# Input projections of a gated encoder layer: tiles one by one, or two by two as Strassen products

## The reference

```python
h = rms_norm(x, g_pre);  proj = h @ w_in          # 1024 x 7424: 58 tiles of 128 columns
ya = short_gated_conv(a_b, a_c, a_x, w_conv) * silu(a_z);            ua = ya @ w_up_a
yb = window_attention_with_sink(rope(q), rope(k), v) * silu(b_z);    ub = yb @ w_up_b
mk, mv = split(rms_norm(mem, g_mem) @ w_mem_kv)   # mem: 256 tokens
ym = memory_cross_attention(m_q, mk, mv) * silu(m_z);                um = ym @ w_up_m
merged = sigmoid(g0) * ua + sigmoid(g1) * ub + sigmoid(g2) * um
return x + rms_norm(merged @ w_out, g_post)
```

## Time and profile before

| | us |
|---|---|
| median of 3 runs | 1021.28 |
| profiled execution | 1020.34 |
| its span, first to last instruction | 1018.3 |
| TensorE busy | 990.7 |
| VectorE busy | 474.3 |
| ScalarE busy | 347.5 |
| GpSimd busy | 167.6 |

### The profile page before, as it was taken

How to read it: one execution, slowest core, us unless ns; L and a number is a source line. 1 busy time by engine, 2 the same in 40 slices (tenths; PEclk the granted TensorE clock), 3 DMA queues, 4 the chain that set the end, 5 groups by cost and what they waited for, 6 DMA issues and landing times.

```text
span 1018.3 us, 12976 instructions
## 1 busy us (share of the span) xinstructions
PE 990.7 (97%) x4672; PEld 824.7 (81%) x4672; DVE 474.3 (47%) x896; ACT 347.5 (34%) x567; POOL 167.6 (16%) x85
## 2 busy tenths in 40 slices
PE   4999999999999999999999999999999999999997
PEld 3788888888878888888888888888888888887885
DVE  5524322245477777774555544334435312127343
ACT  6321131211365555553320344434422211115121
POOL 1112122121111111111220011121122112210000
PEclk9999999999999999999999999999999999999999
DMA  6322111112111111111121410011111111160322
GB/s 224 107 51 53 62 41 62 41 41 70 32 50 50 50 49 49 49 39 62 41 84 62 135 62 31 31 51 38 44 42 45 49 31 62 31 257 0 124 82 83
DMA packets 21339, 65.41 MB, mean 64 GB/s; under 512 B 3232, under 2 KB 4384, under 8 KB 21056
## 3 DMA queue, kind: packets, MB, share of 16 engines
q1 hardware_dynamic: 20992, 64.39, 19.0%
q10 hardware_dynamic: 320, 0.66, 0.4%
HBM read 56.51 MB, written 4.19 MB: 60 GB/s over the span
## 4 chain that ended last, share of the span: by engine, by line
PE 84%; DVE 7%; ACT 4%; issue 3%; DMA 1%; DVEq 0%; SPq 0%; ACTq 0%
PE pm L377 22%; PE pm L379 22%; PE pm L378 22%; PE pm L617 3%; PE pm L619 3%; PE pm L618 3%; ACT area_a L738 2%; PE sa L466 2%; PE pv L589 1%; PE pm L541 1%; PE sa L573 1%; PE pv L480 1%; DVE area_a L1027 1%; DVE units_r L1034 1%; PE sa L458 1%
## 5 line engine op out<-in xcount | busy, mean ns | idle before, releaser
L377 PE MATMUL pm<-h_hi,units_r 128*128 128x512 f32 x928 | 364.0, 392 | 3.0 <-DVE h_lo L935 2.8
L379 PE MATMUL pm<-h_hi,units_r 128*128 128x512 f32 x928 | 361.7, 390 | 0.0
L378 PE MATMUL pm<-h_lo,units_r 128*128 128x512 f32 x928 | 361.7, 390 | 0.0
L340 POOL TENSOR_TENSOR units_r<-units,units_r 128x1024 fp32r<-128x1024 f32 x80 | 166.4, 2080 | 731.9 <-ACT units_r L638 731.9
L377 PEld LDWEIGHTS pm<-h_hi,units_r 128*128 128x128 f32 x928 | 174.5, 188 | 39.3 <-DVE h_lo L935 3.4
L379 PEld LDWEIGHTS pm<-h_hi,units_r 128*128 128x128 f32 x928 | 174.5, 188 | 36.5
L378 PEld LDWEIGHTS pm<-h_lo,units_r 128*128 128x128 f32 x928 | 174.6, 188 | 35.2
L638 ACT ACTIVATE units_r<-units 128x1024 fp32r<-128x1024 f32 x90 | 91.7, 1019 | 198.1 <-PE pm L379 172.2
L1179 DVE TENSOR_TENSOR area_a<-area_a,pm 128x1024 f32<-128x1024 f32 x15 | 18.3, 1221 | 139.5 <-PE pm L379 139.5
L377 PE MATMUL pm<-y_hi,units_r 128*128 128x512 f32 x192 | 76.9, 401 | 0.0
L379 PE MATMUL pm<-y_hi,units_r 128*128 128x512 f32 x192 | 75.0, 390 | 0.0
(11 more groups left out here) (154 smaller groups left out, 1037.9 us busy)
## 6 DMA issues: line engine op xcount, KB each, us to landing
units<-in_w SPq DMA_DIRECT2D x58, 512.0 KB, 3.3
units<-in_wup SPq DMA_DIRECT2D x24, 256.0 KB, 2.6
area_m<-in_x SPq DMA_DIRECT2D x8, 512.0 KB, 7.0
units<-in_wmem SPq DMA_DIRECT2D x8, 512.0 KB, 3.2
area_a<-in_wout SPq DMA_DIRECT2D x2, 2048.0 KB, 10.5
units<-in_x SPq DMA_DIRECT2D x8, 512.0 KB, 3.9
out<-area_a SPq DMA_DIRECT2D x7, 512.0 KB, 2.9
area_a_r<-area_m SPq DMA_DIRECT2D x16, 128.0 KB, 2.3
```

Source lines behind the costliest of these rows:

```text
L340: nc.gpsimd.tensor_tensor(w_lo[:, p, 0:width], raw[:, p, 0:width], w_hi[:, p, 0:width].bitcast(F32), ALU.subtract).then_inc(lo_made, 1)
L377: pe.matmul(pm[:, p, cols], hi, src_hi[:, k, cols], start=(k == 0), stop=False)
L378: pe.matmul(pm[:, p, cols], hi, src_lo[:, k, cols], start=False, stop=False)
L379: mm = pe.matmul(pm[:, p, cols], lo, src_hi[:, k, cols], start=False, stop=(k == chunks - 1))
```

## The change

The 58 tiles are taken in 29 pairs. For a pair, the weights are a 2x2 arrangement of blocks (A11, A12: first tile, two halves of the 1024 inputs; A21, A22: second tile), and the transposed h is 2x2 as well (B11, B21, B12, B22; 512 by 512 each). Instead of the 8 block products, 7 are made (Winograd's form of Strassen's scheme): P1 = A11 B11, P2 = A12 B21, P3 = S4 B22, P4 = A22 T4, P5 = S1 T1, P6 = S2 T2, P7 = (A11 - A21) T3, with S1 = A21 + A22, S2 = S1 - A11, S4 = A12 - S2 and T1 = B12 - B11, T3 = B22 - B12, T2 = B22 - T1, T4 = B21 - T2. A product is 4 blocks x 3 = 12 matmuls. So:

- At the start seven combinations of h (`hc`) are made and split in place of `h_hi` and `h_lo`; VectorE makes the 16 sums, ScalarE the high parts, GpSimd and VectorE the low parts by turns.
- For each pair VectorE makes the four sums of weight blocks (L1201, L1203, L1209, L1217; 128x512, from SBUF to SBUF). The program before has no such sums; in a sibling of this design, which isn't shown here, they were on GpSimd.
- ScalarE and GpSimd split one block of 128x512 per product into a ring of four (`ring`); the products take the four half-banks of `pm` in turn. VectorE puts the four result blocks together with seven additions out of `pm` (`take_c11` to `take_c12`; ScalarE copies P1 out).
- Results no longer go straight to their consumer. 18 pairs (z, gates, memory queries) are stored to a buffer in HBM, and rotated q and k, and the attention's outputs too; they are read back when they are needed.
- The order is new: pairs 0 to 2 are q, k and v; 18 pairs follow, over 16 of which the 16 attention groups are laid; then 16 steps for the memory's keys and values, then 8 pairs of the convolution with the 8 blocks of the cross-attention between them; then all 24 up products without anything between them (the gates are read back), and the output product as before. All loops are written out.

```diff
-    for step in range(first, last):                       # product(), 48 matmuls a tile
-        half, k = divmod(step, chunks)
-        pe.matmul(pm[:, p, cols], hi, src_hi[:, k, cols], start=(k == 0), stop=False)
-        pe.matmul(pm[:, p, cols], hi, src_lo[:, k, cols], start=False, stop=False)
-        mm = pe.matmul(pm[:, p, cols], lo, src_hi[:, k, cols], start=False, stop=(k == chunks - 1))
+    for k in range(HC):                                   # product(), 12 matmuls
+        pe.matmul(bank, hi, moving_hi(k), start=(k == 0), stop=False)
+        pe.matmul(bank, hi, moving_lo(k), start=False, stop=False)
+        mm = pe.matmul(bank, lo, moving_hi(k), start=False, stop=(k == HC - 1))
+    order = [(0, "P1"), (0, "P2"), (1, "P1"), (1, "P2")]
+    order += [(p, name) for p in range(2) for name in ("P6", "P7", "P4", "P5", "P3")]
+    for p in range(2, PAIRS):
+        if p == P_CONV: order += [("m", i) for i in range(M_STEPS)]
+        order += [(p, name) for name in ("P1", "P2", "P6", "P7", "P4", "P5", "P3")]
+    # PE, before each product: its bank is free of the product four before
+    pe.wait_ge({"P1": a_made, "P2": c11, "P6": b_made, "P7": c_made, "P4": c21, "P5": d_made,
+                "P3": c12}[earlier], before + 1)
+    # DVE, slot by slot
+    elif name == "P2":  take_c11(p); softmax_head(gr) ...; take_cross(i - 1); cross_max(i)
+    elif name == "P7":  add_p7(p); rotate / make_values / softmax_tail(gr) / cross_norm(i)
+    elif name == "P4":  take_c21(p); sums_first(p + 1); sum_s2(p + 1)
+    elif name == "P5":  take_c22(p); take_probs(gr) / cross_take(i)
+    elif name == "P3":  take_c12(p); sum_s4(p + 1); conv_taps(p) if i in (0, 2, 4)
+    # ACT, after product n: the high part of product n + 4; POOL: its low part
+    at_least(act, slot_done, n - RING + 1)
+    nc.scalar.activation(ring[:, n % RING, 0, :], operand(n), ACT.Copy).then_inc(hi_made, 1)
+    nc.gpsimd.tensor_tensor(ring[:, n % RING, 1, :], operand(n), ring[:, n % RING, 0, :].bitcast(F32),
+                            ALU.subtract).then_inc(lo_made, 1)
```

More of the change, by code:

```diff
@@ L436, in conv_tile, with turn_v @@
-            def conv_tile(j, q, first=0, last=None):
-                product(2 * j + (T_CONV + q) // 2, q % 2, KC, h_hi, h_lo, 4 * j + (T_CONV + q + 1), first, last)
-            with pe.Fori(0, AC - 1) as j:
-                for q in range(4):
-                    conv_tile(j, q)
-            def scores(i, g):
+            def turn_v(half):
+                pe.wait_ge((c11, c12)[half], 3)
+                if half == 0:
+                    pe.wait_ge(h_copied, 2 * KC)
+                for b in range(4):
+                    mm = pe.transpose(sa[:, half, b * P:(b + 1) * P], raw_block(2, 0, half)[:, b * P:(b + 1) * P],
+                                      ident[:, :])
+                mm.then_inc(v_turned, 1)
@@ L625, in _ @@
-            out_block(0, 1)
-            with pe.Fori(1, NB // 2 - 1) as i:
-                for p in range(2):
-                    out_block(i, p)
-            out_block(NB // 2 - 1, 0)
-            out_block(NB // 2 - 1, 1, last=True)
+                        hi, lo = mb[:, p, 0, k, :], mb[:, p, 1, k, :]
+                        wo = wo_of[half]
+                        pe.matmul(dst, hi, wo[:, k, 0, :], start=(k == 0), stop=False)
+                        pe.matmul(dst, lo, wo[:, k, 0, :], start=False, stop=False)
@@ L633, in _ @@
+                        mm = pe.matmul(dst, hi, wo[:, k, 1, :], start=False, stop=(k == KC - 1))
+                    if half == 0 and b == NB - 1:
+                        mm.then_inc(out_half_done, 1)
+                mm.then_inc(out_done, 1)
+            for b in range(NB):
+                out_block(b)
         @block.scalar
         def _(act):
[L635 to L638 removed]
@@ new lines, in _ @@
+            for g in range(UPS):
+                gate_sigmoid(g)
+                if g >= 1 and g + 3 < UPS:
+                    high_part(NS + g + 3)
+                if y_step(g) is not None:
+                    y_tile(y_step(g))
+                if wo_step(g) is not None:
+                    wo_high(wo_step(g))
+            act.wait_ge(merged_done, 2 * KC - 1)
+            merged_high(0, 0, KC - 1)
+            act.wait_ge(merged_done, 2 * KC)
+            merged_high(0, KC - 1, KC)
+            merged_high(1)
@@ L888, in _ @@
-            with act.Fori(1, NB // 2 - 1) as i:
-                for p in range(2):
-                    out_block(i, p, True)
-            out_block(NB // 2 - 1, 0, False)
-            out_block(NB // 2 - 1, 1, False, last=True)
         @block.vector
@@ L1261, in _, with out_block @@
+            for g in range(UPS - 1):
+                if y_step(g) is not None:
+                    y_tile(y_step(g))
+                if wo_step(g) is not None:
+                    wo_low(wo_step(g))
+                gate_up(g)
+            merged_low(0, 1, 0, KC - 1)
+            wo_low(wo_step(UPS - 1))
+            last_gate_up(0)
+            last_gate_up(1)
+            merged_low(0, 2, KC - 1, KC)
+            merged_low(1, 3)
             dve.wait_ge(gpost_landed, 16)
-            def out_block(i, p, more, last=False):
+            def out_block(b):
+                p, last = b % 2, b == NB - 1
```

2012 lines of the change are left out of this document (1194 added, 818 removed).

## The result

| | median us | range | runs | span of the profiled run | against before (95%) |
|---|---|---|---|---|---|
| before | 1021.25 | 1020.91 to 1022.86 | 4 | 1018.3 | |
| changed | 1054.07 | 1052.69 to 1056.01 | 4 | 1054.2 | 1.0320 (1.0297 to 1.0342) |

The account below looks back on a forecast made before the run. The kernel was taken as bound by TensorE's number of matmuls. -78.9 + 35 + 10 + 2 + 12 + 6 - 2 (waits that go) = -16 gave 1005 us against 1021.25 before, range 968 to 1034.

Parts of the forecast that it names:

- What goes, -78.9: Products of all 29 pairs: seven in place of eight take 348 matmuls of 0.2268 us away, -78.9 us.
- The price of a sum: VectorE's sums of weight blocks: 0.69 us each, up to 1.98 if one meets a GpSimd low part.
- The start, +35: Start to the first attention scores: 62 us not spent on matmuls against 27 today, +35 us (bounds +15 and +50).
- the mark of 160: First attention scores, forecast at about 144 us: before 125 or after 160 would show the forecast wrong.
- The attention, +10: Attention groups: an addition ahead of the first mask makes TensorE wait 0.6 us 16 times, +10 us (0 to +21).
- The memory steps, +2: Sixteen memory steps of about 1.4 us against GpSimd's 1.29, hardly any cover, +2 us (0 to +6).
- Convolution, +12: Convolution pairs with cross-attention: query splitting behind VectorE's taps, scores 2.5 to 3.5 us late three times, +12 us (0 to +30).
- The up products, +6: The 24 up products: VectorE's gating and y tiles exceed some products, one product of slack takes most, +6 us (0 to +20).
- VectorE as the bound (1034): Rival, attention and convolution pairs: VectorE's sums and scalings meet low parts and it becomes the bound, 1034 us; chance 0.16.
- The gain whole (969): Rival, whole kernel: hand-offs are hidden, start +20 and all others together +7, 969 us; chance 0.22.
- The half clock: Rival, start: after idle stretches nine products run at 0.42 us a matmul, +13 us, 1018; chance 0.08.
- The traffic: Rival, DMA: share rises from 19.0% to about 35%, each gate 1 us late, 1029 us; chance 0.09.

Follow-up runs that it names:

- e_mem: Changed kernel with the memory's root, scaling, transposes and splits one or two products earlier in their engines' lists; 1047.46 us.
- e_mq: Changed kernel with VectorE staging the next cross read's queries ahead of the convolution's taps in even convolution pairs; 1038.71 us.
- e_y: Changed kernel with first gates and y tiles loaded ahead of the last cross store, and VectorE's last cross read-out ahead of the last convolution tile; 1037.56 us.
- e_thin: Changed kernel with the four sums of weight blocks cut to 64 of 512 columns from pair 1 on; 1044.25 us.
- e_best: Changed kernel with e_mem, e_mq, e_y, e_low, an earlier start read-out, branch M's y tiles at 9, 10, 12, 14, and an earlier ScalarE high part; 1008.20 us.
- e_warm: Changed kernel with filler matmuls ahead of pair 0's second product (16) and sixth product (36); 1053.94 us.
- e_low: Changed kernel with the ten low parts of combined inputs that GpSimd makes at the start moved to VectorE; 1050.31 us.
- e_spread: Changed kernel with the four y tiles of branch M worked at up products 9, 11, 13, 15 instead of 9 to 12; 1055.81 us.

## Why the prediction was wrong, by its steps

- **What goes, -78.9: right.** 348 matmuls are gone, and those that are left stand 0.227 us apart in the middle.
- **The price of a sum: right.** 0.98 us on the mean, between 0.69 and 1.98. S4 meets a low part nearly always (1342 ns), S2 never (683). GpSimd was busy for 384.8 us, not 350, as its low parts took 1.41 us on the mean and not 1.29.
- **The start, +35: too small, about +52**, and at 160.8 the first scores crossed the mark of 160 that I had set. Pair 0's P6 started at 54.1 (forecast 53), its P5 at 75.0, not 68. The addition L1227 stood behind the last low parts, as I had said, but these took 1.70 us each beside GpSimd's, and TensorE waited 7.7 us for it. So pair 0 ended at 82.2, not 73. What was left of pair 1 then took 13.4 us, with no wait, where I had put 22. Pairs 2 and 3 took 27.8 and 27.5, not 22: ScalarE's high part for the second product stands behind a rotation's cast there, with waits of 5.8 and 4.9 us. Before the first scores came 4.3 us more for the load of the keys.
- **The attention, +10: nearly right.** The mask waits are 3.1 us in 15, not 0.6 x 16; a pair takes 23.7.
- **The memory steps, +2: wrong, about +14.** I looked at low parts against steps, not at what prepares the memory ahead of them. That is a chain VectorE, TensorE, VectorE (L1380, L728, L1388) with 3.0 + 2.9 + 3.3 us of waits. The granted clock was lower behind the first and the last of them (0.66 from 548 to 553 us, 0.52 from 566 to 573) and 1.00 behind the second. e_mem gave 7.0 of it back.
- **Convolution, +12: mechanism right, size off.** Three times, as said, behind the taps, 2.8 to 3.1 us late. But each cost 4.6 to 5.0 us, because the clock fell behind it. About +19 in all; e_mq gave 14.5 back, and the rest lies in the last pair, 27.9 us long, which no run took apart.
- **The up products, +6: the step that failed.** "One product of slack takes most of it" did not look at SyncE's list: the loads of gates and y tiles are queued behind the last cross store, which waits for the tail of VectorE's convolution. It measured about +33. Some 20 of them lie in the gaps at the first five products, and e_y gave 17.3 back by the order of two lists, SyncE's and the end of VectorE's. The four tiles of branch M cost 8.9 in the changed kernel (12.7 in e_y), and the first block of the output product 3.5. I had put the mark at 15 us of waits for gates and tiles; it was 22.5.
- **The rivals.** VectorE as the bound (1034) is refuted as a mechanism: there is no wait for banks in the attention, e_thin's gain is confined to three pairs, and e_best is fast with nearly the same load. The gain whole (969) did not come. The half clock did come. In the first 160 us the granted clock was 0.88 (windows), but 42 matmuls of products stood 0.42 us apart there, three and a half products and not nine: 8.4 us at most, of which e_warm took back 2 at P2 without a gain. What the others cost at the start is open. It came also where I had not looked, behind waits of about 3 us in the later stages. The traffic came to 35.6% as said. That it did not bind is argued, not shown by a run with less of it: e_y moves the same data and is faster, as it asks for it earlier.

What made the sign wrong is that I priced waits inside stages and took most transitions as covered. Four terms came out 17 + 12 + 7 + 26 too low, and only the attention's 7 too high. What stays open: the 154.1 - 81.6 = 72 us at e_best's start that no product fills, and how early the rotation's chain could be.

## What to carry to other kernels

When work on the bound engine shrinks, walk every queue at every change of stage, the one that issues the loads first: ask what each load stands behind, not only how long it takes. An instruction that the next stage waits for belongs ahead of one that only fills time on the same engine; the three largest mends here are such swaps and add no work. Judge a change of form only after that: here the same form was 3.2% slower or 1.3% faster, by the order of its lists and by the engine of ten low parts.

## What the runs showed of the hardware

- **Elementwise work on GpSimd stretches VectorE's work out of SBUF, not that on PSUM.** 687 ns became 1191 for a scaling of 128x384 with the sums on GpSimd; the masks out of PSUM stayed at 553. The Trainium skill (SBUF — State Buffer, SBUF: two separate sides) calls the pair of ports that the two share an exclusive lock, held for a whole instruction; the row of 4.51 us beside three GpSimd instructions agrees. Moving 116 sums of about 1.37 us to GpSimd took only 53 us off VectorE, whose sums had been 113 us. Low parts on both engines side by side took 1.7 us each; on VectorE with GpSimd at work only now and then 0.81 to 0.89 (e_low: 13.03 us for 16, 3.56 for 4).
- **A wait of about 3 us can cost more than its length.** Waits of 2.8 to 3.1 us ahead of the cross scores cost 4.6 to 5.0, and one of 3.6 us inside an up product cost 5.4 (e_spread): the granted clock falls to its lower level and some of the matmuls behind the wait stand 0.42 us apart. A wait of 1.2 us at the same place cost 1.5, at a granted clock of 1.00 (e_thin). Not every longer wait brings it down: behind 2.9 us at 558 to 561 us of the changed kernel it stayed at 1.00. The Trainium skill (TensorE: Matmul & The Clock Gate, Part 1) has idleness bring the throttled state back; the 0.56 behind 2.83 us of wait agrees, now in the middle of a kernel.
- In e_warm 2.5 us without a matmul, after 8 us of them at full clock, came before a stretch of five us with a granted clock of 0.66.
